# A decoder step on one core: the last halves of the out-projection leave GpSimd, and gate/up's first two units go by token halves

## The reference

```python
hn = rms_norm(h, norm1_g);  z = hn @ w_in            # conv gates, conv value, q, k, v
y  = concat(rms_norm(gated_conv(z)), rms_norm(attention(z)))
h  = h + y @ w_out                                   # out-projection, 2048 x 2048
hn = rms_norm(h, norm2_g)
h  = h + (silu(hn @ w_gate) * (hn @ w_up)) @ w_down  # 2048 -> 5632 -> 2048
out = rms_norm(h, final_norm_g)
```

## Time and profile before

| | us |
|---|---|
| time, median of 3 runs | 2096.91 (2094.72 to 2098.84) |
| the profiled execution: its own time | 2096.93 |
| its span (first to last instruction) | 2095.4 |
| PE busy | 2053.9 |
| DVE busy | 1411.8 |
| ACT busy | 822.1 |
| POOL busy | 317.1 |

### The profile page before, as it was taken

One profiled execution on the slowest core, in us unless ns is written; L12 is line 12 of the kernel. 1 busy time (PEld: TensorE's weight loads), 2 busy tenths in 40 slices (PEclk: granted clock), 3 DMA queues, 4 the chain that ended last, 5 costly groups with the idle time before them and its releaser, 6 DMA issues.

```text
span 2095.4 us, 41528 instructions
## 1 busy us (share of the span) xinstructions
PE 2053.9 (98%) x16965; PEld 2025.6 (97%) x16965; DVE 1411.8 (67%) x1664; ACT 822.1 (39%) x1148; POOL 317.1 (15%) x292
## 2 busy tenths in 40 slices
PE   7999999999999899999999999999999999999997
PEld 6999999999999899999999999999999999999997
DVE  6753535354644797877877777777777877787765
ACT  4232323234222354444444444444445444444431
POOL 5112121423566500000000000000000000000025
PEclk9999999999999999999999999999999999999998
DMA  8422222232444243343343443433337543834332
GB/s 263 146 81 81 80 78 80 79 108 71 126 138 139 93 142 128 124 151 120 123 151 109 140 139 122 140 114 127 110 120 269 158 121 86 270 91 121 103 130 82
DMA packets 301099, 264.75 MB, mean 126 GB/s; under 512 B 7182, under 2 KB 278134, under 8 KB 300808
## 3 DMA queue, kind: packets, MB, share of 16 engines
q1 hardware_dynamic: 292496, 244.21, 37.6%
q0 software_dynamic: 3360, 12.47, 1.7%
q10 hardware_dynamic: 5160, 6.88, 0.9%
HBM read 230.17 MB, written 35.45 MB: 127 GB/s over the span
## 4 chain that ended last, share of the span: by engine, by line
PE 95%; DVE 3%; DMA 1%; POOL 1%; issue 0%; ACT 0%; ACTq 0%; DVEq 0%; POOLq 0%
PE pu L1008 39%; PE pu L713 23%; PE pa L1008 18%; PE pu L1086 4%; PE pa L713 4%; PE pa L1086 2%; PE pa L816 1%; PE pu L836 1%; PE pu L746 1%; PE pa L825 1%; DVE a_lo L1762 0%; DMA g_fin<-final_norm_g 0%; PE pa L1165 0%; DVE w_lo L1655 0%; DMA cvs<-conv_w 0%
## 5 line engine op out<-in xcount | busy, mean ns | idle before, releaser
L1008 PE MATMUL pu<-X,w_hi 128*128 128x260 f32 x4592 | 843.9, 283 | 2.2 <-DVE X L1977 2.2
L1008 PEld LDWEIGHTS pu<-X,w_hi 128*128 128x128 f32 x4592 | 717.2, 189 | 2.6 <-issue 2.3
L1008 PE MATMUL pu<-X,w_lo 128*128 128x260 f32 x2296 | 649.5, 283 | 0.0
L1008 PEld LDWEIGHTS pu<-X,w_lo 128*128 128x128 f32 x2296 | 433.5, 189 | 0.1
L1008 PE MATMUL pa<-X,w_hi 128*128 128x260 f32 x2160 | 405.4, 282 | 0.0
L1008 PEld LDWEIGHTS pa<-X,w_hi 128*128 128x128 f32 x2160 | 340.6, 188 | 0.0
L1008 PE MATMUL pa<-X,w_lo 128*128 128x260 f32 x1080 | 305.0, 282 | 0.0
L713 PE MATMUL pu<-a_hi,w_hi 128*128 128x260 f32 (+2 forms) x1312 | 270.7, 288 | 0.7 <-ACT cvs L1250 0.5
L713 PE MATMUL pu<-a_lo,w_hi 128*128 128x260 f32 (+2 forms) x1312 | 265.6, 284 | 0.0
L713 PE MATMUL pu<-a_hi,w_lo 128*128 128x260 f32 (+2 forms) x1312 | 265.0, 283 | 0.0
L1205 ACT ACTIVATE w_hi<-w_raw 128x1024 fp32r<-128x1024 f32 x112 | 112.4, 1051 | 312.7 <-PE pu L713 148.5
(11 more groups left out here) (293 smaller groups left out, 2824.8 us busy)
## 6 DMA issues: line engine op xcount, KB each, us to landing
w_raw<-w_gate SPq DMA_DIRECT2D x44, 1024.0 KB, 5.2
raw_b<-w_up SPq DMA_DIRECT2D x42, 1024.0 KB, 5.1
w_raw<-w_in SPq DMA_DIRECT2D x72, 512.0 KB, 4.9
w_raw<-w_down SPq DMA_DIRECT2D x48, 512.0 KB, 5.1
w_raw<-w_out SPq DMA_DIRECT2D x32, 512.0 KB, 4.1
w_raw<-w_down SPq DMA_DIRECT2D x16, 1024.0 KB, 5.8
f_t<-fbuf SPq DMA_DIRECT2D x42, 260.0 KB, 2.1
t_t<-tbuf SPq DMA_DIRECT2D x16, 520.0 KB, 4.0
```

The source lines that it names most:

```text
L1008: last = mm(bank, w_slot(w, slot)[:, P * j:P * j + P], X[:, 2 * X_REGION[x] + lo, HT * j:HT * j + HT], start=start and j == 0 and i == 0, ...
```

## The change

GpSimd's `project_half` is gone. DVE's `evacuate_half` does both adds itself and counts `rh_made` to 4. ACT squares each half into a buffer of its own (`square_half`), and `norm_half` on PE sums `acc` of the first 14 tiles and the two squares with three ones-matmuls. SP issues the four stores. The second pair of evacuations comes after unit 1's first two splits on DVE.

Units 0 and 1 go by token halves: first half of unit 0, first half of unit 1, second half of 0, second half of 1. `norm_half(1)` stands before unit 1's third product. On PE the half of unit 1 waits for `half_free` 4 and `root_made` 4 + h. Unit 1's split weights lie where `x1` and `x2` will be, and these two are made once unit 1's products have read them (`g_done` 14 and 16), `x6` after `b12` has been read (`g_done` 14). `t2` is kept in place of n22, and the orders on ACT and DVE are written anew. On ACT, unit 0's first two silus, `x5`, two splits of unit 2, the other two silus and two more splits stand between `b12` and `x4`:

```diff
@@ after load_pair(0) on SP
+            def store_half(i):
+                part = slice(HT * (i // 2), HT * (i // 2) + HT)
+                sp.wait_ge(s.rh_made, i + 1)
+                sp.dma_start(t["x_t"][14 + i % 2][:, part], res[:, 14 + i % 2, part]).then_inc(h_half[i % 2][i // 2], 16)
+            store_half(0)
+            store_half(1)
             load_pair(1, 1, 0, 0, [(s.g_lo, 2), (s.g_lo, 4)])
+            store_half(2)
+            store_half(3)
             load_pair(2, 0, 1, 0, [(s.g_lo, 6), (s.g_lo, 8)])
             load_pair(3, 1, 1, 1, [(s.x_lo, 16), (s.x_lo, 16)])
@@ norm_half(h) on PE
-                mm(pa[:, h, 0:HT], ones[:, :], acc[:, HT * h:HT * h + HT], start=True, stop=True).then_inc(s.ss_done, 1)
+                pe.wait_ge(s.rh_square, 2 * h + 2)
+                pe.wait_ge(s.half_free, 2 * h + 1)
+                for i, sq in enumerate((acc, half_sq[0], half_sq[1])):
+                    last = mm(pa[:, h, 0:HT], ones[:, :], sq[:, part], start=i == 0, stop=i == 2)
+                last.then_inc(s.ss_done, 1)
@@ plain units on PE
-            for u in range(2):
-                plain_unit(u)
+            for h in range(2):
+                for u in range(2):
+                    plain_half(u, h)
@@ orders on ACT
+            square_half(0, 0)
+            square_half(1, 0)
             scale_half(0, 0)
             root_half(0)
...
             plain_hi(0, 3)
+            plain_hi(1, 0)
+            plain_hi(1, 1)
+            square_half(0, 1)
+            square_half(1, 1)
+            plain_hi(1, 2)
+            plain_hi(1, 3)
+            root_half(1)
             scale_half(0, 1)
-            root_half(1)
             scale_half(1, 1)
-            for name in ("b12", "x5", "x1"):
-                x_hi(name)
+            x_hi("b12")
...
+            for name in ("x4", "x1", "x2"):
+                x_hi(name)
@@ fast_unit on ACT, after the copy of u2
+                if isinstance(u, int) and u == 2:
+                    x_hi("x6")
@@ evacuate_half on DVE
+                dve.tensor_tensor(t_c[:, part], t_c[:, part], t_a[:, part], ALU.add).then_inc(s.rh_sum, 1)
+                dve.wait_ge(s.rh_sum, i + 1)
+                dve.tensor_tensor(res[:, x, part], t_c[:, part], x_res[:, slot, part], ALU.add).then_inc(s.rh_made, 1)
@@ order on DVE
             invert_half(0)
-            evacuate_half(0, 1)
...
             plain_lo(0, 3)
+            plain_lo(1, 0)
+            plain_lo(1, 1)
+            evacuate_half(0, 1)
+            evacuate_half(1, 1)
+            plain_lo(1, 2)
+            plain_lo(1, 3)
             invert_half(1)
...
             x_sum("t1")
...
             sum1(2, 1, 0)
             sum3(2, 0)
             form_lo(2, 0, 0)
             form_lo(2, 0, 1)
             sum2(2, 0)
-            x_lo("x6")
+            x_sum("t3")
+            x_sum("t2")
             form_lo(2, 0, 2)
             form_lo(2, 0, 3)
+            for name in ("x4", "x1", "x2"):
+                x_lo(name)
             sum4(2, 0)
+            form_lo(2, 0, 4)
+            x_sum("t4")
+            form_lo(2, 0, 5)
+            x_lo("x6")
```

More of the change, by code:

```diff
@@ L90, in slot_free_count @@
     if isinstance(u, int) and u == 2:
[L91 removed]
+        return 8 + 1 + f
     return prod_count(u - 1, (4, 5, 6, 3)[f])
[L95 removed]
+X_SRC = {"n11": 0, "n21": 1, "n12": 2, "n22": 3, "t1": 4, "t3": 5, "t2": 6, "t4": 7}
 X_REGION = (0, 4, 5, 1, 6, 3, 2)
[L97 removed]
+X_MADE = {0: 0, 3: 1, "b12": 2, 5: 3, 4: 4, 1: 5, 2: 6, 6: 7}
 G1, G2, GCA, CW = 0, 16, 32, 48
@@ L372, in w_slot, with plain_slot @@
             return w[:, slot // 2, 1024 * (slot % 2):1024 * (slot % 2) + 1024]
+        def plain_slot(u, i, lo):
+            return X[:, 8 + 2 * (i // 2) + lo, 1024 * (i % 2):1024 * (i % 2) + 1024] if u else w_slot((w_hi, w_lo)[lo], i)
         def tiles8(ap):
@@ L461, in build @@
                  [pu[1][:, 1, 0:HT], pa[:, 0, 0:HT], pa[:, 1, 0:HT]]]
-        cbank = [[pu[0][:, 0, 0:HT], pu[0][:, 1, 0:HT], pu[1][:, 0, 0:HT], pu[1][:, 1, 0:HT]],
-                 [pa[:, i, 0:HT] for i in range(4)]]
+        cbank = [[pu[i % 2][:, i // 2, 0:HT] for i in range(4)], [pa[:, i, 0:HT] for i in (0, 2, 1, 3)]]
+        half_sq = [u_buf, cy]
         s = Semaphores(lambda name: ctx.enter_context(nc.semaphore(name)))
@@ L970, in norm_half @@
             def norm_half(h):
[L972 to L975, removed]
+                part = slice(HT * h, HT * h + HT)
+                pe.wait_ge(s.acc_added, 38)
+                pe.wait_ge(s.rh_square, 2 * h + 2)
                 pe.wait_ge(s.half_free, 2 * h + 1)
-                mm(pa[:, h, 0:HT], ones[:, :], acc[:, HT * h:HT * h + HT], start=True, stop=True).then_inc(s.ss_done, 1)
+                for i, sq in enumerate((acc, half_sq[0], half_sq[1])):
+                    last = mm(pa[:, h, 0:HT], ones[:, :], sq[:, part], start=i == 0, stop=i == 2)
+                last.then_inc(s.ss_done, 1)
             def project_half(h, slot):
@@ L998, in _, with product @@
                 project_half(1, slot)
-            PASSES = [(w_hi, 0), (w_lo, 0), (w_hi, 1)]
-            def product(bank, slot, x, start, waits=()):
+            PASSES = [(0, 0), (1, 0), (0, 1)]
+            def product(bank, slot, x, start, waits=(), weight=None):
+                wt = weight or (w_slot(w_hi, slot), w_slot(w_lo, slot))
                 for j in range(8):
@@ L1006, in product, with plain_half @@
                         pe.wait_ge(sem, count)
-                    for i, (w, lo) in enumerate(PASSES):
-                        last = mm(bank, w_slot(w, slot)[:, P * j:P * j + P], X[:, 2 * X_REGION[x] + lo, HT * j:HT * j + HT],
+                    for i, (low, lo) in enumerate(PASSES):
+                        last = mm(bank, wt[low][:, P * j:P * j + P], X[:, 2 * X_REGION[x] + lo, HT * j:HT * j + HT],
                                   start=start and j == 0 and i == 0, stop=j == 7 and i == 2, skip_group_check=True)
                 last.then_inc(s.g_done, 1)
-            def plain_unit(u):
+            def plain_half(u, h):
                 banks = cbank[u]
                 if u == 1:
[L1016 to L1021, removed]
+                    pe.wait_ge(s.half_free, 4)
+                    pe.wait_ge(s.root_made, 4 + h)
+                for i in range(4):
+                    b, x, start = 2 * h + i % 2, ((0, 3), (6, 5))[h][i // 2], i < 2
+                    if h == 0:
+                        pe.wait_ge(s.g_lo, 4 * u + i + 1)
                     if u == 0 and start:
-                        pe.wait_ge(s.half_free, (1, 3, 2, 4)[b])
-                    if u == 0 and i == 2:
+                        pe.wait_ge(s.half_free, b + 1)
+                    if u == 1 and h == 0 and i == 2:
                         norm_half(1)
                     ready = 2 * X_MADE["b12" if x == 6 else x]
-                    product(banks[b], slot, x, start,
-                            [[(s.x_lo, ready + 1)], [(s.x_lo, ready + 2)]] if u == 0 else ())
+                    product(banks[b], i, x, start, [[(s.x_lo, ready + 1)], [(s.x_lo, ready + 2)]] if u == 0 else (),
+                            (plain_slot(u, i, 0), plain_slot(u, i, 1)))
             def fast_unit(u, g, kind):
@@ L1178, in _ @@
             turn_y(KT - 1)
-            for i, (sq, done, n_sq) in enumerate([(acc_d, s.acc_added, 55), (u_d, s.last_squared, 1)]):
+            for i, (sq, done, n_sq) in enumerate([(acc_d, s.acc_added, 53), (u_d, s.last_squared, 1)]):
                 pe.wait_ge(done, n_sq)
@@ L1396, in plain_hi @@
             def plain_hi(u, i):
[L1398 to L1401, removed]
+                act.wait_ge(s.unit_done, U_P3 - 1 if u == 0 and i < 2 else U_P3)
                 act.wait_ge(graw[0][i // 2], 16 * (u + 1))
-                act.activation(tiles8(w_slot(w_hi, i)), block_of(w_raw, i // 2, i % 2), ACT.Copy).then_inc(s.g_hi, 1)
+                act.activation(tiles8(plain_slot(u, i, 0)), block_of(w_raw, i // 2, i % 2), ACT.Copy).then_inc(s.g_hi, 1)
             def form_hi(u, g, kind, f):
@@ L1418, in x_hi @@
                 i, k, tt, src, made = X_FORM[name]
-                if name == "x6":
-                    act.wait_ge(s.g_done, 8 + 6)
+                if name in ("x1", "x2", "x6"):
+                    act.wait_ge(s.g_done, 16 if name == "x2" else 14)
                 for h in range(2):
@@ L1428, in scale_half @@
                 act.wait_ge(h_half[slot][h], 16)
[L1429 to L1432, removed]
+                act.wait_ge(s.rh_square, 2 * h + slot + 1)
                 r = res[:, x, HT * h:HT * h + HT]
@@ L1443, in _, with square_half @@
             scale_res(13, 1, 6)
+            def square_half(slot, h):
+                part = slice(HT * h, HT * h + HT)
+                act.wait_ge(s.rh_made, 2 * h + slot + 1)
+                act.activation(half_sq[slot][:, part], res[:, 14 + slot, part], ACT.Square).then_inc(s.rh_square, 1)
+            square_half(0, 0)
+            square_half(1, 0)
             scale_half(0, 0)
```

(13 more changed lines are left out.)

31 lines of the change are left out of this document (14 added, 17 removed).

## The result

The changed kernel takes 2102.9 us (median of 13 runs, 2097.81 to 2105.1) where the kernel before took 2099.13 beside it (13 runs, 2094.72 to 2102.13). The ratio is 1.0018, with a 95% interval from 1.0011 to 1.0025: 3.8 us slower by the medians, where 3.5 was forecast.

A forecast was written before the change was run, and what follows sets the result against it. PE, busy for 98% of the span, was taken as the bound, with DVE just behind. Unit 3's later start (+0.95 us) and the clock's fall (+2.6) on 2096.93 gave 2100.4 us; range 2094 to 2103, the forecast's own 2098.6 to 2102.2.

The forecast's parts named there:

- The sum: Whole kernel: +0.95 us for unit 3 starting later and +2.6 us for the lower clock, on 2096.93, giving 2100.4 us.
- The first part's gain: PE up to unit 2: the old waits of 1.5, 2.2 and 4.0 us shrink or go; unit 2 starts 6.3 us earlier.
- DVE without GpSimd: DVE's pairs after the first half-norm: no longer slowed to 2.94 and 3.35 us by GpSimd, saving 3.0 us.
- The table load: ScalarE between Squares and roots: a possible table switch, making the first root 0.8 us later, was left out.
- The load: raw_b for unit 3: issued at 770.7, 3.7 us later than before, because x6 moves down; complete at 779.2.
- PE's stand: Before unit 2's last product: PE waits 7.3 us for c22; unit 3 starts at 785.2 at full clock, 0.95 us later.
- The clock: After PE's long wait in unit 2: the granted clock falls to 0.50 and costs 2.6 us.
- the stretch of 17 to 20: A half-clock stretch of 3 us in the old trace, taken to bound the clock's loss below at 1.4 us.
- The stores: Stores moved from GpSimd's queue to SP's: no cost, each 130 KB store landing in 2.1 us.
- The gain stays: Rival, unit 2: raw_b complete before 772.0, product 6 does not wait, time 2090.6 us; chance 0.13.
- The short stand: Rival, unit 2: raw_b complete 2 to 2.6 us earlier, clock loss 0 to 2.6, time 2095.3 to 2097.9; chance 0.18.
- The clock falls earlier: Rival: PE's 1.2 and 1.4 us waits lower the clock, second norm up to 2.6 us later, up to 2103.0; chance 0.12.

The follow-up runs named there:

- x_load: The changed kernel with t2 and t4 kept elsewhere and made earlier, so the raw_b loads wait for the sums, not all sixteen half-tiles; ratio 0.9996 to the kernel before.
- x_clock: The changed kernel with 48 unread matmuls on PE in its long wait before unit 2's last product; ratio 0.9998 to the kernel before.
- x_both: The changed kernel with x_load's early load, and c11, c22 and unit 3's first two splits ahead of sum1(3) and sum3(3) on DVE; ratio 0.9980 to the kernel before.
- x_part1: The kernel before with only GpSimd's project_half moved to DVE, ACT and PE, old order of units 0 and 1; ratio 0.9983 to the kernel before.
- x_lclk: x_load with 16 unread matmuls on PE in its wait before unit 2's last product; ratio 0.9985 to the kernel before.

## Why the prediction was right

**The sum.** The difference came as forecast, 3.8 us for 3.5, from the two terms that made it up (below). The absolute time did not: 2102.9 us is 2.5 over the forecast of 2100.4, over the forecast's own range (to 2102.2) and only just under the top of the whole one (2103). Most of that comes from where the sum started, 2096.91, the median of three runs of the kernel before; thirteen gave 2099.13, 2.2 us more. With that offset the time came close to leaving the range; that it lies inside is in part luck.

**The first part's gain.** Right. PE has no wait before the first half-norm. The waits came as 0.9 us at `x3` (forecast 1.2), 1.0 at unit 1's start (1.4) and 0.4 at `b12` (0.45); none is listed at `x0` (0.1). A half-norm with three ones-matmuls lasts 1.33 us on the chain, forecast 1.38. Unit 2 starts at 758.76; 757.9 was forecast on the old trace's time, which is 758.7 on this one's.

**DVE without GpSimd.** Right. In the timeline of DVE above, the pairs at 703.61 and 707.05 take 2.39 us, where they took 2.94 and 3.35 beside GpSimd. The Trainium skill (SBUF — State Buffer, § Who interferes with whom) says that `tensor_tensor` with both inputs in SBUF contends with GpSimd's reads; the trace agrees, with 2.39 us once GpSimd has stopped.

**The table load.** Leaving it out was right. The trace after has one `ACT_TABLE_LOAD` in the stretch, at Silu, and none between the Squares (0.42 us each, forecast 0.5) and the roots:

```profile
735.46 1.28 ACT L1499 ACT_TABLE_LOAD   x1
```

By the rule of the Trainium skill (ScalarE: Activation LUTs, § Table sets: the hidden batching unit) there would have been a switch if Square stood outside Sqrt's set; this trace has none between them.

**The load.** Right. It is issued at 771.37, forecast 770.7 plus the 0.8 us by which this execution is late. The median to landing is 6.7 us in the DMA issues (6.6 in the earlier trace rows), and from the issue to the end of the chain's DMA piece, 780.01, it is 8.6 (8.5). Two small errors cancel in this: the second load is issued 0.4 us behind the first, not 0.6, and takes 8.2 us, not 7.9. DVE's idle time is 4.60 us, forecast 4.6. x_load shows that this condition was the cause: only the condition, the places of two sums and their turn in DVE's list were changed, and DVE's wait for the load was gone.

**PE's stand.** Right: 7.1 us for 7.3, released by `c22`. At full clock unit 3 would start at 783.19 + 2.87 = 786.06, on the old clock 785.27, where 785.2 was forecast. So the term is +1.0 for +0.95.

**The clock.** Right in kind, and in size within what the runs resolve: 2.7 us by x_clock (8.68 less 6.00), 2.6 forecast. The lower bound taken from the stretch of 17 to 20 (1.4) was not met behind the long stand, though x_load's 1.5 behind a short one came close to it.

**The stores.** Right in that they cost nothing: no wait of PE in the stretch is for one. A store took 3.2 us to land (median of four), where 2.1 was forecast from GpSimd's queue.

**The rivals.** *The gain stays* needed the load 7 us sooner. It did not hold for this change, but x_both shows that much of the gain was there to keep, 4.6 us of the 6.3, and x_part1 gains 3.8 with the first part alone. *The short stand* fell: the second load took no less than its rows said, and DVE's chain was not ahead. The lower end of its price, no loss of clock behind a stand of about 5 us, would not have come either, for x_load had a stand of only 2.4 us and still paid 1.5. *The clock falls earlier* fell: the stands of 0.9 and 1.0 us left it at 1.00.

What stays open is why a stand of 2.2 us left the clock at 1.00 in the kernel before, and one of 2.4 us in x_load did not: the two differ in place and in what PE did ahead of them, and no run here varies the length alone. Whether the second part alone would lose more than it does together with the first was not tried.

## What to carry to other kernels

A step that is moved down takes with it whatever waits on it, here a load whose buffer lies over data that only the last tile releases: follow the semaphore from the moved step to the queue, and from the queue to the first consumer of the transfer, and put the operations that do not need it (here `c11`, `c22`) ahead of it in that engine's list. An earlier stage gains only if every later due time moves with it. Count a stand of PE in a full stream for more than its length: here the lower clock behind it cost 1.5 us after 2.4 us and 2.7 us after 7.1, while behind stands of 0.9, 1.0 and 2.2 us the clock stayed at 1.00. Where the stand can't be removed, matmuls that nobody reads got that part back (x_lclk, x_clock).

## What was not expected of the hardware

Behind a stand of 2.4 us the granted clock fell (0.57 over two microseconds, x_load), when behind one of 2.2 us it had not. A stand's price in clock was 1.5, 2.5 and 2.7 us behind 2.4, 4.3 and 7.1 us. Sixteen matmuls into an unread bank, ahead of the last 0.5 us of that stand, were enough to keep it at 1.00.
